# A two-layer decoder step: x loaded and normed by tiles at the opening, and the norms after the experts moved beside the last gathers

## The reference, cut to what matters

```python
def _rmsnorm(x, g):
    y = x * lax.rsqrt(jnp.mean(x * x, axis=-1, keepdims=True) + EPS)
    return y * g

def _layer(x, l, ...):
    h = _rmsnorm(x, norm_mix[l])
    parts = h @ w_in[l]                  # DeltaNet, window attention, pooling, gates
    x = x + merged @ w_out[l]
    return x + _peer(_rmsnorm(x, norm_ffn[l]), ...)

for l in range(2):
    x = _layer(x, l, ...)
y = _rmsnorm(x, norm_final)
```

## Time and profile before

| | us |
|---|---|
| median of 3 runs | 5286.22 |
| lowest, highest | 5284.10, 5288.55 |
| the profiled execution, device time | 5288.41 |
| the profiled execution, span | 5286.6 |

### The profile page before, as it was taken

One profiled execution on the slowest core, in us unless ns is written; L12 is line 12 of the kernel. 1 busy time (PEld: TensorE's weight loads), 2 busy tenths in 40 slices (PEclk: granted clock), 3 DMA queues, 4 the chain that ended last, 5 costly groups with the idle time before them and its releaser, 6 DMA issues. The chain is left out here.

```text
span 5286.6 us, 50111 instructions
## 1 busy us (share of the span) xinstructions
PE 4599.7 (87%) x17270; PEld 2669.8 (51%) x17270; DVE 3010.7 (57%) x7288; ACT 1238.8 (23%) x3105; POOL 1551.2 (29%) x1420
## 2 busy tenths in 40 slices
PE   7899999998988777877699999999988997878776
PEld 5766677754444323332178667777544443323221
DVE  5523323247677799965465232322476667999654
ACT  2211211022222233321122122110222222333211
POOL 0412100014444444443204121000244444444442
PEclk9999999999999999999999999999999999999999
DMA  2223243349999999999812232432599999999997
GB/s 104 80 74 112 74 136 95 106 158 415 404 415 398 420 420 419 420 419 420 343 61 81 82 117 69 139 123 80 200 414 405 409 401 420 420 420 420 419 420 305
DMA packets 338776, 1432.11 MB, mean 271 GB/s; under 512 B 27548, under 2 KB 156438, under 8 KB 190602
## 3 DMA queue, kind: packets, MB, share of 16 engines
q0 software_dynamic: 177376, 1268.07, 59.1%
q1 hardware_dynamic: 158238, 160.41, 9.6%
q10 hardware_dynamic: 2908, 0.43, 0.0%
HBM read 1400.18 MB, written 49.44 MB: 274 GB/s over the span
## 5 line engine op out<-in xcount | busy, mean ns | idle before, releaser
L2748 PE MATMUL ps<-early,diag 128*128 128x512 f32 (+1 forms) x3648 | 1729.7, 623 | 388.0 <-ACT diag L2661 387.6
L2563 POOL DMA_INDIRECT early<-in_peer,ids x912 | 1009.8, 1107 | 1811.3 <-PE ps L2748 1269.4
L2748 PEld LDWEIGHTS ps<-early,diag 128*128 128x128 f32 (+1 forms) x3648 | 674.6, 192 | 1392.7 <-issue 741.4
L2591 DVE SCALAR_TENSOR_TENSOR early<-early,rows 128x1024 f32<-128x1024 f32 x912 | 1101.5, 1223 | 398.5 <-DMA early<-in_peer,ids 397.1
L2748 PE MATMUL ps<-late,diag 128*128 128x512 f32 (+1 forms) x960 | 466.7, 633 | 130.7 <-ACT diag L2661 130.3
L2661 ACT ACTIVATE diag<-consts_sb,weight 128x128 f32<-128x128 f32 (+1 forms) x1152 | 392.8, 388 | 680.1 <-DVE weight L2601 666.6
L2653 ACT ACTIVATE gel<-dot 128x2 f32<-128x2 f32 x576 | 117.3, 204 | 1262.0 <-DVE early L2591 964.6
L1270 PE MATMUL ps<-hT,gate_ring 128*128 128x288 f32 x1536 | 395.9, 412 | 11.1 <-ACT gate_out L1281 8.3
L2748 PEld LDWEIGHTS ps<-late,diag 128*128 128x128 f32 (+1 forms) x960 | 175.0, 191 | 420.2 <-ACT diag L2661 220.3
L2591 DVE SCALAR_TENSOR_TENSOR late<-late,rows 128x1024 f32<-128x1024 f32 x240 | 289.9, 1222 | 116.7 <-DMA late<-in_peer,ids 116.1
L2563 POOL DMA_INDIRECT late<-in_peer,ids x240 | 257.8, 1074 | 328.3 <-PE ps L2748 315.4
(11 more groups left out here) (380 smaller groups left out, 5380.5 us busy)
## 6 DMA issues: line engine op xcount, KB each, us to landing
gate_ring<-in_w_in POOLq DMA_DIRECT2D x48, 512.0 KB, 4.8
slot<-in_w_branch SPq DMA_DIRECT2D x16, 1152.0 KB, 6.4
ring<-in_w_in SPq DMA_DIRECT2D x8, 2048.0 KB, 9.2
late<-in_peer_query SPq DMA_DIRECT2D x32, 512.0 KB, 7.9
early<-in_peer,ids POOLq DMA_INDIRECT x912, 18.5
gate_rows<-gate_out POOLq DMA_DIRECT2D x48, 288.0 KB, 2.4
slot<-gate_rows SPq DMA_DIRECT2D x16, 864.0 KB, 8.3
slot<-in_w_in SPq DMA_DIRECT2D x6, 2048.0 KB, 11.0
```

Source lines behind the costliest of these rows:

```text
L2563: pool.indirect_dma_start(place(q), None, table_rows, bass.IndirectOffsetOnAxis(ap=ids[:, n, c:c + 1], axis=0)).then_inc(s.pair[PLACE[q]], 16)
L2591: nc.vector.scalar_tensor_tensor(out=up, in0=up, scalar=1.0, in1=rows[:, n, :], op0=ALU.mult, op1=ALU.mult, accum_out=dot[:, i % 2, k:k + ...
L2748: ins = nc.tensor.matmul(g.ps[0:r, 2 * (n % 2) + m, :], diag[:, q % DIAGS, 0:r], place(q)[:, D + m * 512:D + (m + 1) * 512], start=False, ...
```

## The change

1. **Opening.** x comes in five transfers, each with a semaphore of its own; behind them on SP's queue come slab 0, the constants without the identity, and slab 1. ACT issues gamma and the identity (64 KB). Nothing waits for all of it: each tile is squared, rooted, scaled, turned and copied as it lands, with mean and root made for each tile; half of the copies to `hT` goes to DVE. The first projection waits for slab 0 alone, its block 10 for the constants.
2. **Norm after the experts.** The class `NextNorm` takes the place of `norm_stage`, and runs within the loop over groups. With `NEXT_AT` = 260: ACT squares tiles 0 to 3 in groups 260 to 263, DVE makes the four means in group 265, ACT the roots in 266, DVE scales a tile in groups 268, 270, 272 and 274. If a layer follows, PE turns these tiles in groups 270 to 276, ahead of the group's sums, and ACT and DVE copy a half each behind their work of that group. Only tile 4 stays for the end: ACT squares it and DVE copies it to `g.x` straight from PSUM in two halves, crosswise.
3. **Transfers.** Gamma is loaded behind the doubling of tile 4's indices. Slabs 0 and 1 of the next layer are issued when 572 and 574 of the 576 pairs are summed. In the last layer y is stored by tiles, as each is scaled; the sample tile in two halves.
4. `EXTENDED` becomes 212, so that the last four pairs use places 8 to 11, which don't overlap the slabs. The clearing of the experts' semaphores moves to `delta_in`. The blocks of `norm_stage` and of the final store are gone.

```diff
+def opening(nc, g, t, places):
...
+            for n in range(TILES):
+                src = t["x_prompt"][0, n * P:(n + 1) * P] if n < 4 else t["x_sample"].rearrange("b t d -> (b t) d")
+                sp.dma_start(g.x[0:ROWS[n], n], src).then_inc(s.x_in[n], 16)
+            sp.dma_start(*places.first_slab(0)).then_inc(s.in_slab[0], 16)
+            sp.dma_start(g.consts[:, rest[0]], t["consts"][:, rest[0]]).then_inc(s.consts_in, 16)
+            sp.dma_start(*places.first_slab(1)).then_inc(s.in_slab[1], 16)
...
+        def _(act):
+            act.dma_start(gam[:], t["norm_mix"][bass.ds(0, 1)].broadcast_to([P, D])).then_inc(s.loaded2, 16)
+            act.dma_start(g.consts[:, known], t["consts"][:, known]).then_inc(s.loaded, 16)
...
+            for n in range(TILES):
+                r = ROWS[n]
+                act.wait_ge(s.x_in[n], 16)
+                if n:
+                    act.wait_ge(s.squared, n)
+                nc.scalar.activation(junk[0:r], g.x[0:r, n], ACT.Square, accum_out=ss[0:r, n:n + 1]).then_inc(s.squared, 1)
+                if n >= 2:
+                    turned(n - 2)
+                act.wait_ge(s.mean_in, n + 1)
+                nc.scalar.activation(ss[0:r, n:n + 1], ss[0:r, n:n + 1], ACT.Sqrt).then_inc(s.rooted, 1)
...
+                dve.wait_ge(s.squared, n + 1)
+                link(nc.vector.tensor_scalar(root, root, 1.0 / D, EPS, ALU.mult, ALU.add))
+                nc.vector.reciprocal(root, root).then_inc(s.mean_in, 1)
+                if n >= 2:
+                    turned(n - 2)
+                dve.wait_ge(s.rooted, n + 1)
...
+                nc.vector.scalar_tensor_tensor(out=rows[0:r, n], in0=g.x[0:r, n], scalar=root, in1=gam[0:r], ...)
...
-EXTENDED = 27 * EARLY
+EXTENDED = 212
...
+class NextNorm:
...
+    def sync(self, sp):
+        sp.dma_start(self.gam[:], self.gamma.broadcast_to([P, D])).then_inc(s.next_gamma, 16)
+        if self.hT is None:
+            for n in range(LAST_TILE):
+                sp.wait_ge(s.next_rows, n + 1)
+                sp.dma_start(self.o["y_p"][0, n * P:(n + 1) * P], self.rows[:, n]).then_inc(s.y_stored, 16)
...
+        else:
+            for i in range(2):
+                sp.wait_ge(s.downs_done, PAIRS - 4 + 2 * i)
+                to, src = self.places.first_slab(i)
+                sp.dma_start(to, src).then_inc(s.in_slab[i], 16)
...
+    def scalar(self, act, i):
+        at = i - NEXT_AT
+        if 0 <= at < LAST_TILE:
...
+            act.wait_ge(s.x_copied, at + 1)
+            nc.scalar.activation(self.junk[:], g.x[:, at, :], ACT.Square, accum_out=self.ss[:, at:at + 1]).then_inc(s.next_squared, 1)
+        if at == LAST_TILE + 2:
+            act.wait_ge(s.next_mean, 1)
+            nc.scalar.activation(self.ss[:, 0:LAST_TILE], self.ss[:, 0:LAST_TILE], ACT.Sqrt).then_inc(s.next_rooted, 1)
+        n, late = divmod(at - 10, 2)
+        if self.hT is not None and 0 <= n < LAST_TILE and not late:
+            act.wait_ge(s.next_turned, n + 1)
+            self.copy_half(nc.scalar.copy, n, 0)
...
+    def last_scalar(self, act):
+        nc.scalar.activation(self.spare[:, 2:3], self.ss[:, 0:1], ACT.Sqrt).then_inc(s.square_half, 1)
+        act.wait_ge(s.summed, TILES)
+        act.wait_ge(s.square_half, 1)
+        for a in range(2):
+            if a:
+                act.wait_ge(s.x_half, 1)
+                act.wait_ge(s.square_half, 2)
+            nc.scalar.activation(self.junk[0:NS, 0:512], g.ps[0:NS, self.bank(a), :], ACT.Square, accum_out=self.spare[0:NS, a:a + 1]
+                                 ).then_inc(s.square_half, 1)
+        act.wait_ge(s.next_mean, 2)
+        root = self.ss[0:NS, LAST_TILE:TILES]
+        nc.scalar.activation(root, root, ACT.Sqrt).then_inc(s.next_rooted, 1)
...
+    def last_vector(self, dve, link):
+        dve.wait_ge(s.summed, TILES)
+        for a in (1, 0):
+            if a == 0:
+                dve.wait_ge(s.square_half, 2)
+            nc.vector.tensor_copy(g.x[0:NS, LAST_TILE, a * 512:(a + 1) * 512], g.ps[0:NS, self.bank(a), :]).then_inc(s.x_half, 1)
+        dve.wait_ge(s.square_half, 3)
+        link(nc.vector.tensor_tensor(root, self.spare[0:NS, 0:1], self.spare[0:NS, 1:2], ALU.add))
+        link(nc.vector.tensor_scalar(root, root, 1.0 / D, EPS, ALU.mult, ALU.add))
+        nc.vector.reciprocal(root, root).then_inc(s.next_mean, 1)
+        dve.wait_ge(s.next_rooted, 2)
...
+        for a in range(2):
+            self.scale(LAST_TILE, slice(a * 512, (a + 1) * 512))
...
@@ score_expert_stage
+            following.sync(sp)
...
+                following.vector(dve, link, i)
+            following.last_vector(dve, link)
...
-            copy_x(TILES - 1)
+                following.scalar(act, i)
+            following.last_scalar(act)
...
+                following.tensor(pe, i)
                 for k in range(GROUP):
                     q = i * GROUP + k
                     pe.wait_ge(s.diagonal, q + 1)
```

More of the change, by code:

```diff
@@ L209, in __init__ @@
         self.pool_stored = keep("pool_stored")
+        self.consts_in = keep("consts_in")
+        self.x_in = [keep(f"x_in{n}") for n in range(TILES)]
+        self.in_slab = [keep(f"in_slab{i}") for i in range(2)]
         self.delta_stored = keep("delta_stored")
@@ L298, in clear_single @@
         pool.sem_clear(range(first, last + 1))
-def norm_stage(nc, g, gamma, rows, sb, transposed=True, sources=()):
+IDENT_AT = CONST["ident"][0]
+def opening(nc, g, t, places):
     s = g.s
+    sb = places.inner.above()
+    rows = sb("rows", [P, TILES, D])
     gam, junk, ss = sb("gam", [P, D]), sb("junk", [P, D]), sb("ss", [P, 8])
[L306 to L368, removed]
@@ L431, with __init__, first_slab, delta_stage @@
 EXT_S = CONV - 1 + SEQ
-def delta_stage(nc, g, t, o, l, slab):
-    w_in = layer(t["w_in"], l)
[L436 to L446, removed]
+class DeltaPlaces:
+    def __init__(self, g, t, l):
+        sb = g.space(AT_LATE)
+        self.zT, self.cc = sb("zT", [P, 4, TOK]), sb("cc", [P, 12, TOK])
+        self.vecs, self.ab = sb("vecs", [P, 64]), sb("ab", [P, TILES, 8])
+        self.heads, self.gb = sb("heads", [P, 8]), sb("gb", [P, TILES, 8])
+        self.inner, self.chunks = sb.above(), sb.above()
+        self.ring = self.inner("ring", [P, 2, 4096])
+        w_in = layer(t["w_in"], l)
+        self.slabs = [rows_of(w_in)[:, :, i * 512:(i + 1) * 512] for i in range(4)]
+    def first_slab(self, i):
+        return slab_view(self.ring, i, KT, 512), self.slabs[i]
+def delta_stage(nc, g, t, o, l, slab, places):
+    w_in = layer(t["w_in"], l)
+    p = places
+    delta_in(nc, g, t, o, l, w_in, p.zT, p.cc, p.vecs, p.ab, p.heads, p.ring, p.slabs, p.inner)
     next_semaphores(g)
-    delta_chunks(nc, g, t, o, l, zT, cc, vecs, ab, heads, gb, chunks, slab)
+    delta_chunks(nc, g, t, o, l, p.zT, p.cc, p.vecs, p.ab, p.heads, p.gb, p.chunks, slab)
 NORMED = 2 * H
@@ L478, in _ @@
                     slab_ready(pe, g, u // 4, ahead=2)
+                if u in (0, 4):
+                    pe.wait_ge(s.in_slab[u // 4], 16 * (l + 1))
                 w = slab_view(ring, u // 4, KT, 512)
@@ L502, in _ @@
                 if u == 10:
+                    pe.wait_ge(s.consts_in, 16)
                     pe.wait_ge(s.ab_copied, 2)
@@ L2505, in score_expert_stage @@
+def score_expert_stage(nc, g, t, l, rows, sc, sc0, ids, gates, router, late, w_q, out, sb, store_state, following):
     s = g.s
@@ L2753, in _ @@
                     pe.sem_inc(s.summed, 1)
+            following.last_tensor(pe)
     next_semaphores(g)
@@ L2838, in build @@
             out = Output(nc, g, t, l, oc, merge, rows, late)
[L2839 to L2848 removed]
+            score_expert_stage(nc, g, t, l, rows, sc, sc0, ids, gates, router, late, w_q, out, ffn, lambda sp: store_pool(sp, g, o, l, new),
+                               NextNorm(nc, g, t, l, o, rows, columns[l + 1], places[l + 1]))
 TABLES = ("peer_up", "peer_down")
```

172 lines of the change are left out of this document (145 added, 27 removed).

## The result

The changed kernel takes 5254.6 us (median of 4 runs, 5252.9 to 5256.3), the kernel before 5285.9 beside it: a ratio of 0.994, 95% interval 0.9923 to 0.9958, so it is faster by about 0.6%. The forecast was 5258 in 5249 to 5268, faster with 0.93. The profiled execution took 5252.9, its span is 5251.1; that is 35.5 us less than the profiled execution of before, while the medians are 31.3 apart.

A forecast was written before the change was run, and what follows sets the result against it. DMA gathers, paced by one lagging engine, bound the expert stages; the norms leave most engines idle. Savings of 10.8 (opening), 7.9 (between layers) and 9.8 us (end) sum to 28.5, giving 5258 us, range 5249 to 5268.

The forecast's parts named there:

- rival (c): Loop over groups has no slack: each added instruction costs its own length, making the kernel slower, 5298 us; chance 0.04.
- (d): Waits in ACT's and DVE's work order pass idle time on; gaps shrink only a few us: 5284 us; chance 0.03.
- Opening: Start to first projection: falls from 34.2 to 22.0 us, saving 12.2 before the clock's loss.
- The clock's 1.4: Opening: half clock as the first projection begins takes back 1.4 us, bounds 0 and 2.9.
- Gap: Between the layers: layer 2's projection starts 4.9 us after layer 1's last sum, instead of 18.4.
- Clock between the layers: Layer 2's projection runs its first 5.8 us at half clock, costing 2.9 us.
- Gamma: Expert stages: loading gamma among the gathers costs 2.0 us a layer.
- y's stores: Layer 2's expert stage: storing 2.1 MB of y among the gathers costs 5.1 us.
- rival (a): Moved bytes of gamma, y and slab cost nothing on the slow DMA engine: 5248 us; chance 0.14.
- Slab 0: End of layer 1's experts: early slab transfer delays the last gather by 0.7 us, bounds 0 and 5.0.
- rival (b): Slab ahead of last gather, cold clock at both starts, late tile 0: gain 20 to 22, 5265; chance 0.21.
- End: After layer 2's last sum: 6.6 us to the span's end, instead of 23.5.

The follow-up runs named there:

- warm: Changed kernel plus three PE matmuls of 128x512 between layer 1's last sum and tile 4's transposes; 5254.5 us (one run).
- best: Changed kernel with y's stores held back to the last gathers, three PE matmuls between the layers, root table loaded before the first square; 5247.1 us.
- gamma5: Changed kernel with gamma loaded five times in a row in each expert stage; 5261.5 us (one run).
- slab_end: Changed kernel with slabs 0 and 1 of layer 2 issued only after all 576 pairs of layer 1 are summed; 5260.0 us (one run).
- the repeat: The kernel before and the changed kernel, both unedited, measured again: 5283.9 and 5255.4 us, ratio 0.9944.
- x_together: Changed kernel with ACT waiting for all five tiles of x before squaring the first; first projection at 27.7 us, 7.5 later.

## Why the prediction was right, and where its terms were off

- **The bound and the mechanism** hold: the idle stretches shrank by about what I gave (43.7 us against 42.6), with tile 4 alone left, and the loop took up all the work of tiles 0 to 3 at no cost. In the four runs without y's stores among the gathers the stage of layer 2 is 1506.4 to 1506.7 us, against 1505.1 to 1506.4 in the kernel before, with scalings, squares and two tables in it. Layer 1 says it more sharply: from the sum of pair 536 to that of pair 560, where PE turns the tiles, 59.8 to 59.9 us pass in all fourteen traces, before and after. The rival (c), no slack, is out, and so is (d). That it is the backlog of gathers which covers PE's turns wasn't tested by itself.
- **Opening**: 14.0 saved against 12.2. Tile 0 was there at 6.4 instead of 7.3, and the chain is 2.05 us a tile on average instead of 2.3: DVE's small operations take 0.15 each, and one of the four steps has no copy in it. Order of the loads (5.7) and awaiting each tile by itself (7.5, with the table) were each priced by a run; what is left of the 14.0 wasn't taken apart. The clock's 1.4 was 0 in this trace. Of the 11 traces of the changed kernel and its variants 4 show a half clock at the opening, with 22.3 to 22.4 us for the first 41 pairs against 20.7, which is 1.6 to 1.7. The forecast's 1.4 was half of a bound and met neither case.
- **Gap**: 5.6 instead of 4.9. Up to the scaling the sum holds within 0.1; what I undersized is the way from the second half's scaling to hT (0.78 to the copy, forecast 0.35) and the block's end (0.60, forecast 0.3). Some 0.2 of it is the half clock, which takes in tile 4's transposes: the gap was 5.4 in the traces in which they ran at the full one (`warm`, `best`, `gamma5`).
- **Clock between the layers**: 2.1 against 2.9; the half clock covered 4.2 us of the projection, not 5.8. Eight traces give 1.6 to 2.6.
- **Gamma**: 1.3 a layer, forecast 2.0: the mis-sized term. I added to its bytes the slow first 3 us of the norm stage. But transfers that started with no gamma were slow at first as well (`slab_end`, 296 GB/s), and in the loop the 16 engines were moving already.
- **y's stores**: 4.8 against 5.1; the moved bytes cost their time, so rival (a) is out.
- **Slab 0**: 0.1 against 0.7. The mechanism of this term, turns piece by piece, is wrong: 2 MB issued beside the last two gathers delayed them by 0.1 to 0.2 us in every run. The single DMA records of the trace after say more. The slab's first piece starts 1.0 us after the issue, at 2618.26, and of the gathers only the last one's eight pieces of 8 KB are still to come. They start 0.31 us apart, as the pieces before them do, up to 2620.6, with no room for a slab's piece between them. Then one engine ends its share of the slabs 2 us after the others, in pieces of 2 KB every 0.08 us; in `slab_end` none does. The records don't name the engine; that it is the slow one follows from the spacing. On it, then, the last gather went first and the slab behind it, which is the forecast's bound of 0. The Trainium skill (DMA: Bandwidth & Descriptors, Queues, rings and completion order) says that an engine drains a whole packet of one queue before it turns to the next. The trace agrees as far as nothing came between the eight pieces; the estimate of 1 to 2.6 us by that rule, for which a slab's packet had to go ahead of them, isn't borne out. What decides the order isn't shown. The slab's part of rival (b) is out with it, and so is its late tile 0; the cold start came in 4 of 11 traces.
- **End**: 6.5 against 6.6.

Terms as measured: -14.0 - 12.8 - 16.9 for the stretches, + 4.8 + 2 x 1.3 + 0.1 for the transfers, + 2.1 for the clock: -34.1. The medians differ by 31.3 and, in the repeat, by 28.5 (5283.9 to 5255.4), each give or take some 9 us by its interval; the rest is within what the long stretches scatter. The forecast's 28.5 lies closer to both than its terms deserve: they are 5.6 us short of the measured ones, nearly all on the same side, and the long stretches of these traces made up for part of that. That much was luck.

## What to carry to other kernels

Where a stage is bound by DMA, ask of each engine how much it rests in one round of the loop. Here the norm of all finished tiles fitted into that rest, and only the last tile's part of the norm stays on the path. Transfers are another matter: what was moved beside this DMA-bound loop cost its bytes at the loop's full rate, so issue it when the last gathers are under way and only the compute tail is left; y's 2 MB cost 4.8 us in the loop and 0.2 there. And price a moved transfer by its bytes at the rate of the loop it joins, not by the rate of the place that it comes from.

## What the runs showed of the hardware

- The granted clock fell to half (1.2 GHz) in a gap in which PE rested 3.3 us and then had little to do, in all eight traces of it. With three matmuls of 0.94 us in that rest, and 1.06 us of rest left, it fell in both traces. With a longest rest of 0.43 us it stayed whole in the one trace there is. The loss was 1.6 to 2.6 us.
- Isolated stretches of 3.4 us at half clock cost 1.7 us each, and come in some executions of a kernel and not in others (893.0 and 1046.6 above).
- One DMA engine of the 16 is about five gathers behind at the end of both stages. What put it there wasn't tried. Of the slabs issued beside its last gathers, its share came behind the last gather, which was delayed by 0.1 us.
- ACT's table load started as soon as ACT's issues were done, ahead of the single wait of the instruction that needs it (at 1.67, with x landing at 6.4), but behind five waits in `x_together` (at 12.68).
